# A two-block transformer forward in f32: moving four SBUF tensors onto 2048-byte boundaries

## What is computed

```python
# first block
h = rms_norm(x, norm1_w); proj = h @ w_in            # queries, keys, values, gates
o_nsa = nsa_mixer(...)                               # compressed, selected and window attention
o_dn = gated_deltanet(...)                           # chunked linear recurrence, 8 heads
mixed = sigmoid(g0) * (o_nsa @ w_up_nsa) + sigmoid(g1) * (o_dn @ w_up_dn)
x = x + mixed @ w_o
h2 = rms_norm(x, norm2_w)
x = x + (silu(h2 @ w_ffn_gate) * (h2 @ w_ffn_up)) @ w_ffn_down
x = rms_norm(x, norm_f_w)
# second block
h = rms_norm(x, attn_norm_g); proj = h @ w_in_2
y = concat(rwkv7_mixer(...), mla_mixer(...))
x = x + y @ w_out
h = rms_norm(x, ffn_norm_g)
x = x + (silu(conv3(h @ ffn_w_gate) + b) * (h @ ffn_w_up)) @ ffn_w_down
x = rms_norm(x, final_norm_g)
```

## The kernel before

| tensor | start before | mod 2048 | mod 512 | start after | mod 2048 | mod 512 |
|---|---|---|---|---|---|---|
| `hx`, `hr` | 44480 | 1472 | 448 | 45056 | 0 | 0 |
| `ring`, `ringl` | 77248 | 1472 | 448 | 77824 | 0 | 0 |
| `high` | 101824 | 1472 | 448 | 102400 | 0 | 0 |
| `yT` | 119296 | 512 | 0 | 119872 | 1088 | 64 |
| U | 135680 | 512 | 0 | 138240 | 1024 | 0 |
| inner tiles `axr` (U + 256 words) | 136704 | 1536 | 0 | 139264 | 0 | 0 |
| merged tiles `mixl` (U + 256 words) | 136704 | 1536 | 0 | 139264 | 0 | 0 |
| merged tiles `mixh` | 153088 | 1536 | 0 | 155648 | 0 | 0 |
| high half, first up projection | `mixh` | 1536 | 0 | `mixh` | 0 | 0 |
| high half, second up projection (U + 9776 words) | 174784 | 704 | 192 | 177344 | 1216 | 192 |

## Time and profile before

### The profile page before, as it was taken

The page is one execution under the profiler, slowest core; times in us unless marked ns, Lnnn a source line. Parts: engine busy times, 40 slices in busy tenths (PEclk is TensorE's granted clock), DMA queues, the critical chain, the costliest instruction groups (busy, mean ns, idle before and its releaser), DMA issues.

```text
span 2854.1 us, 41789 instructions
## 1 busy us (share of the span) xinstructions
PE 2791.8 (98%) x16404; PEld 2428.2 (85%) x16404; DVE 2051.3 (72%) x3158; ACT 1363.8 (48%) x2043; POOL 479.0 (17%) x526
## 2 busy tenths in 40 slices
PE   8999999999999999999999999999989999999998
PEld 7888888888888888888888888878778888888887
DVE  7987787766766666656657889878777777667655
ACT  6453455455554544444446545434354444434434
POOL 2111011110111111001002734511021111001101
PEclk9999999999999999999999999999999999999999
DMA  6444334455555555555556433321445555555555
GB/s 227 163 156 162 112 124 131 144 190 187 192 186 191 187 190 190 188 190 192 188 179 212 162 112 128 101 67 52 148 146 187 191 187 190 191 190 188 192 177 162
DMA packets 132243, 474.63 MB, mean 166 GB/s; under 512 B 14672, under 2 KB 14928, under 8 KB 131792
## 3 DMA queue, kind: packets, MB, share of 16 engines
q1 hardware_dynamic: 132048, 471.96, 50.0%
HBM read 469.80 MB, written 2.10 MB: 165 GB/s over the span
## 4 chain that ended last, share of the span: by engine, by line
PE 89%; DVE 5%; ACT 3%; POOL 1%; issue 1%; DMA 0%; SPq 0%; DVEq 0%; ACTq 0%; POOLq 0%
PE ps L893 88%; DVE ringl L1859 1%; DVE U L1859 1%; ACT high L1399 1%; POOL U L2540 1%; DVE xT L1859 1%; PE ps L896 1%; ACT hr L1399 0%; ACT U L1399 0%; POOL U L2613 0%; DVE U L1868 0%; ACT U L1412 0%; DMA xT<-in_x_dram 0%; DVE hx L1859 0%; DVE U L2056 0%
## 5 line engine op out<-in xcount | busy, mean ns | idle before, releaser
L893 PE MATMUL ps<-hr,high 128*128 128x512 f32 x4672 | 1508.0, 401 | 19.4 <-DVE ringl L1859 17.2
L1859 DVE TENSOR_TENSOR ringl<-ring,high 128x1024 fp32r<-128x1024 f32 x880 | 1080.5, 1230 | 424.5 <-ACT high L1399 423.8
L1399 ACT ACTIVATE high<-ring 128x1024 fp32r<-128x1024 f32 x880 | 914.4, 1041 | 635.8 <-PE ps L893 626.5
L893 PEld LDWEIGHTS ps<-hr,ringl 128*128 128x128 f32 x4672 | 880.0, 188 | 205.6 <-issue 1.4
L893 PE MATMUL ps<-hr,ringl 128*128 128x256 f32 x4672 | 920.6, 278 | 0.0
L893 PEld LDWEIGHTS ps<-hr,high 128*128 128x128 f32 x4672 | 721.9, 189 | 29.4 <-issue 15.1
L893 PE MATMUL ps<-yur,high 128*128 128x512 f32 x2176 | 684.3, 395 | 10.2 <-DVE xT L1859 6.7
L2540 POOL TENSOR_TENSOR U<-U,rs 128x256 f32<-128x256 f32 x292 | 263.0, 901 | 1701.3 <-DVE U L1859 1682.0
L893 PEld LDWEIGHTS ps<-yur,ringl 128*128 128x128 f32 x2176 | 409.4, 188 | 90.8
L1399 ACT ACTIVATE U<-ps 128x256 f32<-128x256 f32 (+3 forms) x481 | 172.7, 371 | 601.2 <-PE ps L893 575.6
L893 PE MATMUL ps<-yur,ringl 128*128 128x256 f32 x2176 | 430.3, 279 | 0.0
(11 more groups left out here) (178 smaller groups left out, 1255.0 us busy)
## 6 DMA issues: line engine op xcount, KB each, us to landing
ring<-in_w_dram SPq DMA_DIRECT2D x870, 512.0 KB, 3.3
ring<-in_w_dram SPq DMA_DIRECT2D x32, 256.0 KB, 3.3
xT<-in_x_dram SPq DMA_DIRECT2D x3, 512.0 KB, 8.1
out_dram<-hx SPq DMA_DIRECT2D x3, 512.0 KB, 2.8
cst<-in_cst_dram SPq DMA_DIRECT2D x1, 1374.5 KB, 12.5
yT<-in_lora_dram SPq DMA_DIRECT2D x1, 1024.0 KB, 7.8
xT<-in_x_dram SPq DMA_DIRECT2D x2, 256.0 KB, 4.7
U<-in_lora_dram SPq DMA_DIRECT2D x1, 512.0 KB, 5.8
```

The costliest lines, as they stand in the source:

```text
L893: return e.matmul(out, l, r, start=start, stop=stop)
L1399: return e.activation(out, i, ACT.Copy, scale=scale)
L1859: return e.tensor_tensor(out, a, b, op)
```

## The change

`onto(n, past)` moves the next free place up, in steps of 16 words, until it (or the place `past` words behind it) is a multiple of `n` bytes. It is called before `hx` and before U (for U with 256 words past). `ring_slot` and `high_slot` give the places of slots in ring and `high`; with their tables of zeros they give what the expressions before gave. U becomes 640 words shorter (23296 to 22656 words). Every instruction, its order, its shapes and its waits are as before; line numbers behind the change are higher by up to 15.

```diff
+RING_PAD = [0] * RING
+HIGH_PAD = [0] * HIGH
...
+        def onto(n, past=0):
+
+            while (base + 4 * (place[0] + past)) % n:
+                place[0] += 16
+
+        def ring_slot(m):
+            return (m % RING) * BLK + RING_PAD[m % RING]
+
+        def high_slot(k):
+            return (k % HIGH) * BLK + HIGH_PAD[k % HIGH]
...
         xT_ = sb("xT", 16 * SEQ)
+        onto(2048)
         h_at = place[0]
         hx_ = sb("hx", 32 * SEQ)
         ring_at = place[0]
-        ring = sb("ring", RING * BLK)
-        ringl = sb("ringl", RING * BLK, F32R, at=ring_at)
-        high = sb("high", HIGH * BLK, F32R)
+        ring = sb("ring", RING * BLK + RING_PAD[-1])
+        ringl = sb("ringl", RING * BLK + RING_PAD[-1], F32R, at=ring_at)
+        high = sb("high", HIGH * BLK + HIGH_PAD[-1], F32R)
         rs_ = sb("rs", SEQ + 16)
         y_at = place[0]
         yT_ = sb("yT", 16 * SEQ)
+        onto(2048, 256)
         u_at = place[0]
...
-                        at = (m % RING) * BLK + off
-                        g = (order[m] % HIGH) * BLK + off if m in order else 0
+                        at = ring_slot(m) + off
+                        g = high_slot(order[m]) + off if m in order else 0
```

More of the change, by code:

```diff
@@ L1543, in split @@
                 n = blocks[m][2] * len(blocks[m][3])
-                o, g = (m % RING) * BLK, (k % HIGH) * BLK
+                o, g = ring_slot(m), high_slot(k)
                 e.wait_ge(s_ring[m % RING], 16 * (m // RING + 1))
@@ L1977, in split @@
                 n = blocks[m][2] * len(blocks[m][3])
-                o, g = (m % RING) * BLK, (order[m] % HIGH) * BLK
+                o, g = ring_slot(m), high_slot(order[m])
                 e.wait_ge(hi.sem, hi.after(m))
@@ L2659, in load @@
                 n = blocks[m][2] * len(blocks[m][3])
-                slot = (m % RING) * BLK
+                slot = ring_slot(m)
                 if m >= RING:
```

## The result

The changed kernel is **slower**: 2861.95 us (2860.24 to 2864.01, 8 runs) against 2855.78 us before (2853.53 to 2857.13, 8 runs), a ratio of 1.0023 (95% interval 1.0013 to 1.0033), 6.2 us. The forecast was 2845.

What follows compares the result with a forecast made beforehand. The prediction took PE's matmul pace to bound the kernel: 13.2 us less for hr and 1.4 more for yT make 11.8 less, so 2854.1 - 11.8 + 2.6 gives 2845 us, range 2800 to 2868.

Steps and rivals of the forecast that it cites:

- What bounds the kernel: In full windows time is the number of matmuls times their pace; the other engines lie under PE.
- Modulo 512, not 2048: Crossing 2048-byte boundaries costs nothing visible, so the change was treated as one of addresses modulo 512.
- 579 where it held 574: Sign of a right forecast: matmuls in a full 100 us window of gate and up tiles, after against before.
- Step 1: hr moves from 448 to 0 and takes the 690 pace: 6.6 ns less per four, 13.2 us together.
- Step 2: Weights move from 448 to 0: taken as nothing; bounds a gain of 50 ns and a loss of 15.
- Step 3: yT from 0 to 64 in up and output projections: net 1.4 us more, bounds 0 and 3.
- Step 4: DVE and ACT splits and loads: a tenth slower or faster, PE still covers it; uncovered DVE cost left out.
- Rival C: Distance between moving read and weights counts: hr stays 696.6, down and wo go up to it; 2864 us, chance 0.20.
- Rival D: Nothing moves; the pace hangs on something else that goes with these tensors: 2857 us, chance 0.10.
- START: Theory set up for the experiments: each operand's own place modulo 512 sets the pace.
- Rival B: Weight loads starting on multiples of 512 disturb matmuls less: 6.6 ns on every four, 2826 us, chance 0.23.
- Rival E: Slow pace of three fours in the first up projection holds everywhere: 31 us, 2888 us, chance 0.07.

Runs made afterwards that it cites:

- off64: The changed kernel with hr, U's tiles and yT at 448 modulo 512, ring and high at 384; 2841.28 us, ratio to before 0.9952.
- w448: The changed kernel with only the weights (ring and high) back at 448 modulo 512; 2842.24 us, ratio to before 0.9957.
- y_back: The changed kernel with only yT back at 0 modulo 512; 2859.55 us, ratio to before 1.0016.
- all64: The changed kernel with ring and high at 448, yT at 0 modulo 512, U padded so every main moving read is 64 past its weights; 2840.14 us.
- split_a: The changed kernel with ring at 0, high and hr at 64, U's tiles and yT at 128 modulo 512; 2861.08 us, one run.
- the four kernels above: Weights at 448 with hr at 448 or 0: 696.6 or 690.0 ns a four; weights at 0 with hr at 448 or 0: 693.4 or 696.7.
- map_even: The changed kernel with moving operands at 0 modulo 512 and each slot of ring and high 64 bytes further on; 2866.65 us, one run.

## Why the prediction was wrong

- *What bounds the kernel* held. The full windows stayed full, the splits on DVE and ACT were unchanged, and time was matmuls times pace: 2000 effective fours x 6.6 = 13.2 us was my price for `hr` at 690, and off64 and w448, where `hr` is at 690, are 13.9 and 12.9 us under before.
- *Modulo 512, not 2048* held, but the period is shorter: 256. The sign "579 where it held 574" was misread: the earlier trace rows have 577 and 576, and with `hr` at 690 the windows hold 581 and 582.
- **Step 1 failed**: "the nearest are the tiles that start at 0, and I take their pace". The tiles differed from `hr` in their start and, as weights were at 448 everywhere, equally in their distance from the weights. One row of before could not separate the two; I chose the start. `hr` moved by 64 bytes together with its weights, distance 0 stayed 0, and its gain was 0.0 instead of 6.6 ns a four (13.2 us).
- **Step 2 failed with it**: "I take nothing, since the fast and the slow paces have the same weights". That the weights' place is the same in all rows says that rows cannot price it, not that it has no price. Moving them cost 6.6 ns a four on down and wo (5.5 us by pace) and took away the gain of `hr`; moving them back in w448 is worth 20 us, down, wo and `hr` together.
- *Step 3*, `yT`: the sign of the whole was right, one term had the wrong sign. The second up projection was to gain 10 ns a four, "both halves off, as `hr` had", and went from 706.7 to 711. By pace the step comes to about 2.0 us: 64 fours of the first up projection from 695 (its three slow fours included) to 706.7, 64 of the second by 4, and of the output projection some 60 from 690 to 700 and some 20 to 707. A part of that is hidden where PE waits. Predicted were 1.4. The times of y_back are no check of it, as said above.
- *Step 4* held: the split of a block takes 1250 ns on DVE and 1057 on ACT, as before.
- *Rival C* was the mechanism, with its place (down and wo), its sign and almost its size: 2864 forecast, 2862 measured. I gave it 0.20 because of the second up projection: its first half has the good distance and its second begins when the load should be over, yet it is slow. In before it mixed 64 and 256, which is 0 modulo 256, and all64 shows that the second half counts: there `yT` is at 64 as in before, the high half is brought to 64 too, and the pace is 690. The argument also took the cost of a mixed read to be a sum over its parts: 706 is more than 690 and than 697. split_a shows the same for the other mix, of the two loads: 703.3 at 128 and 64.
- *Rival D* was excluded by the result itself, since down changed its pace. *START* was excluded by off64 and by the four kernels above. *Rival B* in its form, weights on a multiple of 512 disturb less, is excluded: 690.0 with weights at 384 and at 448, 690.1 with them at 0 and `hr` at 320, and 697 with both at 0.
- *Rival E* was right that one set of addresses can have two paces, and wrong in its evidence and its size: the fours of the earlier trace rows are a transition after a switch, and where a whole read has one distance, a multiple of 64, every steady stretch has one pace.

The range ended at 2868 and held the result. The direction was wrong. From the rows at hand the honest state was that start and distance explained 690 and 697 equally well, and that the change alters one and keeps the other; that deserved chances nearer to each other than 0.40 + 0.23 against 0.20.

## What to carry to other kernels

Before believing in an alignment, list for each pace both addresses of the instruction, and look whether a change moves one against the other or both together; if the rows can't tell, give both readings the same weight. Where TensorE streams float32r with a weight load per matmul, try the weights 64 bytes before the moving operand modulo 256, and keep it so for every operand: here it is 0.5% for a few words of padding, and no effect of boundaries of 512 or 2048 bytes was seen. Compare steady stretches in the trace from start to start: the same stretch repeats to 0.1 ns a four there, while the runs scatter by 0.1%. Before a difference of a few us between two runs is put down to a cause, look at the granted clock in windows where PE is not full.

## What was not expected of the hardware

- Where all parts of the reads have one distance, a multiple of 64, the steady pace of a four depends on (moving minus weights) modulo 256 bytes: 690.0 at 64, 693.3 at 192, 696.7 at 0 and 128, and on nothing else of the addresses that was tried.
- The Trainium skill (SBUF — State Buffer, A bandwidth-pool intuition that's wrong (but worth ruling out)) gives TensorE a second, independent read port for weight loads. The runs do not bear out full independence for float32r: the place of the weights alone, modulo 512, changes the pace of the matmuls beside them by 1% (696.7 in the changed kernel, 690.0 in w448).
- That the read of the weights and the moving read meet in some unit of the memory is my reading of this; no run takes the weight loads away, so it is argued and not shown. ACT, DVE and the DMA engines write to ring and `high` as well, and their places moved with the weights in every run; that the pace is even within a block speaks against them, but no run separates them. Nor is it known why 690 and not the 640 ns of the columns is the best: no steady stretch here went below.
- Pace has memory. After a switch from 697 to a good distance it takes three slow fours to find 690 (0.70 to 0.71 us each), in map_even two. At a distance of 32 the same code ran with 579 and with 568 matmuls per 100 us, and mixed reads go at 700 or 706 from the same remainders. Why mixed distances cost more than either of their parts stays open.
